# HGRN2 heads of a one-core decoder step: the norm's sum over squares in two rounded parts, and the sample keys spread on the diagonal by ScalarE in place of GpSimd

## The chip, the cores and the metric

The kernel runs on one core of one Trainium2 chip. The metric is the device time of one execution in microseconds (us). The engines are TensorE (PE in the profile, with PEld for its weight loads), VectorE (DVE), ScalarE (ACT), GpSimd (POOL) and SyncE (SP), which issues most of the transfers.

## What is computed

One decoder layer runs for a prompt of 256 tokens and 8 sample tokens together, 264 columns in all. The part that matters here is the recurrence of the eight HGRN2 heads and the norm over each head's output, cut from the reference:

```python
def _rmsnorm(x, g):
    xf = x.astype(jnp.float32)
    y = xf * lax.rsqrt(jnp.mean(xf * xf, axis=-1, keepdims=True) + EPS)
    return (y * g.astype(jnp.float32)).astype(x.dtype)
...
    # S_t = diag(a_t) S_{t-1} + k_t^T v_t, o_t = q_t S_t
    s_new = (jnp.exp(b_last[..., 0, :])[..., None] * s
             + jnp.einsum('bhsk,bhsv->bhkv', ki * jnp.exp(b_last - b), vi))
...
    o_h, s_h = _gated_recurrence(q_h, k_h, i_h, log_f, s_h0)
    o_h = _rmsnorm(o_h, hgrn_norm).astype(h.dtype) * jax.nn.silu(zg).reshape(B, L, HGRN_HEADS, HGRN_DV)
```

Four GLA heads of the same form (128 keys, 256 values) follow the eight HGRN2 heads (128 keys, 128 values). The projections around them multiply 2048 features by some 39,000 columns of weights.

## The kernel before

All activations lie feature-major: 128 features on the partitions, 264 tokens in the free dimension. A weight tile is 2048 x 128 and is cut into two slabs of 128 x 1024. Each slab passes through a ring of four places: SyncE loads it into `raw`, ScalarE rounds it to float32r in `whi` (`round_slab`, L293), VectorE makes the rest `wlo = raw - whi` (`rest_slab`, L298), and TensorE multiplies it (`multiply`, L310 to L312) with three float32r matmuls per 128 x 128 block: high by high, high by low, low by high. ScalarE's rounding waits until the slab four places earlier has been multiplied (semaphore `slabs_multiplied`), so it stands in a fixed distance ahead of TensorE.

In the heads (`head(H, D)` on every engine, D = 1 for an HGRN2 head and D = 2 for a GLA head) the recurrence of one head is laid between the eight slabs of four weight tiles. The order is written out by hand on each engine, and semaphores tie them. TensorE's order in a head is: slabs 0 to 3 with two transposes between 0 and 1, `outer` (L589, eight matmuls, weights `k_diag`, for the sample tokens' state update), slabs 4 and 5, the scores, slab 6, `prob_v`, and slab 7 with `head_norm` and `state` in its middle. ScalarE's `slab(k)` rounds TensorE's slab k + 2, so its `slab(4)` is TensorE's slab 6 and waits for the end of TensorE's slab 2.

Two places are touched. The first is `k_diag`, a 72 x 8 x 128 float32r tile, in which each of the 8 sample tokens' keys stands on its own row and zeros elsewhere. It is `ks_tok` times the column mask `own_row`:

```python
            pool.tensor_tensor(k_diag[:], keys, on_row, ALU.mult).then_inc(h_sem["k_diag_ready"], 1)
```

The second is `head_norm`: ScalarE squares the head's output from PSUM into `sq` (float32), and TensorE sums over the partitions by a matmul with a tile of ones (L645, float32).

Of the kernel before, what the change touches and what calls it, by code (L numbers as in the profile page):

```python
# [28 lines left out]
P = 128  # L29
# [3 lines left out]
NS_TOK = 8  # L33
TOK = NP_TOK + NS_TOK
# [45 lines left out]
F32 = mybir.dt.float32  # L80
F32R = mybir.dt.float32r
ALU = mybir.AluOpType
ACT = mybir.ActivationFunctionType
# [6 lines left out]
def build(nc, t):  # L90
    ctx = ExitStack()

    def sb(name, shape, dt=F32):
        return ctx.enter_context(nc.sbuf_tensor(name, shape, dt))

    def sem(name):
        return ctx.enter_context(nc.semaphore(name))
# [28 lines left out]
    ones = sb("ones", [P, P])  # L126
# [3 lines left out]
    own_row = sb("own_row", [S_ROWS, NS_TOK])  # L130
# [15 lines left out]
    ks_tok = sb("ks_tok", [S_ROWS, P], F32R)  # L146
    vs_tok = sb("vs_tok", [S_ROWS, GDV], F32R)
    k_diag = sb("k_diag", [S_ROWS, NS_TOK, P], F32R)
# [9 lines left out]
    with nc.sbuf_tensor("gate_w", [RANK, GH * P], F32) as gate_w, nc.sbuf_tensor("rank_z", [RANK, TOK], F32) as rank_z:  # L158
        pass
    S = sb("S", [P, 2, 4, GDV])  # L160
    s_out = sb("s_out", [P, GDV])
    sq = sb("sq", [P, 2, TOK])
    rs = sb("rs", [P, TOK])
    o_f = sb("o_f", [P, 2, TOK])
    squares = o_f
# [5 lines left out]
    DG, TP = bank[4], bank[5]  # L171
    O = bank[6:8]
# [34 lines left out]
    by_engine = {  # L207
        "act": ["v_tok_ready", "s_tok_ready", "lev_exp", "kd_exp", "kd_tok_ready", "sq_ready",
                "ln_rs", "rs_ready", "o_hi_done", "s_out_ready", "sg_abs", "sg_exp", "sg_ln", "sg_sigma"],
        "dve": ["s_parts_ready", "lev_sub", "lev_ready", "kd_ready", "s_new0", "s_new1", "masked", "probs_ready", "sg_ls",  # L210
                "sg_ready", "o_scaled", "o_gated", "o_done"],
        "pe": ["v_turned", "s_turned", "outer0", "outer1", "so_done", "scores_done", "kd_turned",
               "pv_done", "state_done", "ss_done"],
# [2 lines left out]
    h_sem = {n: sem(n) for names in by_engine.values() for n in names}  # L216
# [22 lines left out]
    def now(H):  # L239

        return H + 2

    def before(H):

        return H + 1
# [284 lines left out]
    def _(pe):  # L530
# [26 lines left out]
        for h in range(GH):  # L557
            mm = pe.matmul(GATE_BANKS[h][:, 0:TOK], gate_w[:, h * P:(h + 1) * P], rank_z[:], start=True, stop=True)
# [82 lines left out]

        def head_norm(H, D):
            pe.wait_ge(h_sem["sq_ready"], now(H))
            for d in range(D):
                mm = pe.matmul(DG[:, 0:TOK], ones[:], sq[:, d, :], start=d == 0, stop=d == D - 1)  # L645
            mm.then_inc(h_sem["ss_done"], 1)

        def head(H, D):
# [122 lines left out]
    def _(act):  # L771
# [25 lines left out]
        for k in range(KT):  # L797
            if k in X_PARTS:
                act.wait_ge(x_landed[list(X_PARTS).index(k)], 16)
            for to, of in MIRROR:  # L800
                last = act.activation(a_hi[:, k, to], x_in[:, k, of], ACT.Identity, scale=gains[:, 0, k:k + 1])
# [90 lines left out]
        def head(H, D, next_D):  # L892

            T = 4 * H + T_HEADS
            more = next_D is not None

            def slab(k):
                round_slab(act, T + (1 + k // 2), (T_HEADS + 1 + k // 2) % 2, k % 2)

            def exp_gate():  # L900

                act.wait_ge(tiles_drained, T + D)
                act.wait_ge(h_sem["sg_ready"], before(H))
                e = sgl[:, 0:D, :]
                act.activation(e, sgz[:, 0:D, :], ACT.Abs).then_inc(h_sem["sg_abs"], 1)
                act.wait_ge(h_sem["sg_abs"], now(H))
                act.activation(e, e, ACT.Exp, scale=-1.0).then_inc(h_sem["sg_exp"], 1)

            slab(2)
            slab(3)  # L910
            slab(4)
            if D == 1:
                exp_gate()
            slab(5)
            slab(6)
            if D == 2:
                exp_gate()
            slab(7)
            act.wait_ge(h_sem["kd_turned"], now(H))
            act.copy(kd_tok[:], TP[:, 0:2 * P].rearrange("s (b k) -> s b k", b=2)).then_inc(h_sem["kd_tok_ready"], 1)  # L920
            act.wait_ge(h_sem["pv_done"], now(H))
            act.wait_ge(h_sem["ss_done"], before(H))
            for d in range(D):
                sqd = act.activation(sq[:, d, :], O[d][:, 0:TOK], ACT.Square)
            sqd.then_inc(h_sem["sq_ready"], 1)
            slab(8)

            act.wait_ge(h_sem["sg_exp"], now(H))
            act.activation(sgl[:, 0:D, :], sgl[:, 0:D, :], ACT.Ln, bias=ones[:, 0:1]).then_inc(h_sem["sg_ln"], 1)
            act.wait_ge(h_sem["ss_done"], now(H))  # L930
            act.wait_ge(h_sem["probs_ready"], now(H))
            act.wait_ge(h_sem["o_scaled"], before(H))
            act.activation(rs[:], DG[:, 0:TOK], ACT.Ln, scale=1.0 / (D * P), bias=eps_col[:])\
               .then_inc(h_sem["ln_rs"], 1)
            act.wait_ge(h_sem["state_done"], now(H))
            act.wait_ge(state_stored, 16 * H + 16)
            act.copy(s_out[:, 0:D * P], TP[:, 0:D * P]).then_inc(h_sem["s_out_ready"], 1)
            act.wait_ge(h_sem["ln_rs"], now(H))
            act.activation(rs[:], rs[:], ACT.Exp, scale=-0.5).then_inc(h_sem["rs_ready"], 1)
            act.wait_ge(h_sem["sg_ls"], now(H))  # L940
            act.activation(sgl[:, 0:D, :], sgl[:, 0:D, :], ACT.Exp).then_inc(h_sem["sg_sigma"], 1)
            if more:
                slab(9)
                decays(H + 1)
                turned(H + 1, next_D)
            act.wait_ge(h_sem["o_gated"], now(H))
            k = H if D == 1 else 2 * H - HH
            act.copy(b_hi[:, bass.ds(k, D), :], o_f[:, 0:D, :]).then_inc(h_sem["o_hi_done"], 1)
            if not more:
                slab(9)  # L950
# [140 lines left out]
    def _(dve):  # L1091
# [14 lines left out]
        for k in range(KT):  # L1106
            dve.wait_ge(a_hi_ready, k + 1)
            for to, of in MIRROR:
                last = dve.scalar_tensor_tensor(out=a_lo[:, k, to], in0=x_in[:, k, of], scalar=gains[:, 0, k:k + 1],
                                                in1=a_hi[:, k, to].bitcast(F32), op0=ALU.mult, op1=ALU.subtract)  # L1110
# [118 lines left out]
        def head(H, D, more=True):  # L1229
# [3 lines left out]
            def slab(k):  # L1233
                rest_slab(dve, T + (1 + k // 2), (T_HEADS + 1 + k // 2) % 2, k % 2)

            def m_tile(j):

                par = (T_HEADS + j) % 2
                if D == 1:
                    uses = H + HH if par else 2 * H + (HH + (j == 3))  # L1240
                else:
                    uses = H + HH if par else H + 2 * HH
                to_stage(T + j, par, uses)
# [40 lines left out]
            for l in range(LEVELS // 2, LEVELS):  # L1284
                last = level_operands(l)
# [20 lines left out]
            for l in range(1, LEVELS):  # L1306
# [5 lines left out]
                last = dve.tensor_tensor(to, to, of, ALU.add)  # L1312
                last.then_inc(h_sem["probs_ready" if l == LEVELS - 1 else "masked"], 1)
            slab(7)
            m_tile(2)
            if more:
                dve.wait_ge(h_sem["cum_ready"], now(H + 1))
# [16 lines left out]
            for d in range(D):  # L1334
                gain = head_gain[:, (0 if D == 1 else 1 + d):(1 if D == 1 else 2 + d)]
                last = dve.scalar_tensor_tensor(out=o_f[:, d, :], in0=O[d][:, 0:TOK], scalar=gain, in1=rs[:],
                                                op0=ALU.mult, op1=ALU.mult)
# [102 lines left out]
        for j in range(2):  # L1440
            at = part_of(j)
            last = dve.scalar_tensor_tensor(out=ms[:, at], in0=spare(j), scalar=1.0 / D_MODEL, in1=eps_s2[:, at], op0=ALU.mult,
                                            op1=ALU.add)
# [98 lines left out]
    def _(pool):  # L1542
# [41 lines left out]
        for l in range(1, LEVELS):  # L1584
            for side in range(2):
                last = side_masks(l, side)
# [11 lines left out]
        def head(H, D):  # L1598

            pool.wait_ge(h_sem["kd_ready"], before(H))  # L1600
            pool.wait_ge(h_sem["s_new1"], before(H))
            pool.tensor_copy(cum[:, TOK:TOK + 2], totals[:, :, H])
            pool.tensor_copy(cum[:, 0:TOK], gates[:, H, :]).then_inc(h_sem["cum_ready"], 1)
            pool.wait_ge(h_sem["scores_done"], before(H))
            pool.wait_ge(h_sem["so_done"], before(H))
            pool.tensor_copy(q_b[:], zq[:, H, :])
            k = hk[:, H, :] if D == 1 else zk[:, H - HH, :]
            pool.tensor_copy(k_b[:], k)

            pool.wait_ge(v_landed, 16 * H + 16)  # L1610
            pool.wait_ge(h_sem["s_turned"], before(H))
            for i, src in enumerate([k] + [v_st[:, d, :] for d in range(D)]):
                to = s_feat[:, i, :].rearrange("c (g s) -> c g s", g=3)[:, :, 0:NS_TOK]
                column = src[:, NP_TOK:TOK].rearrange("c (o b) -> c o b", o=1).to_broadcast([P, 3, NS_TOK])
                last = pool.tensor_copy(to, column)
            last.then_inc(h_sem["kq_ready"], 1)

            pool.wait_ge(h_sem["s_parts_ready"], now(H))
            pool.wait_ge(h_sem["outer1"], before(H))
            keys = ks_tok[:].bitcast(F32).rearrange("b (o k) -> b o k", o=1).to_broadcast([S_ROWS, NS_TOK, P])  # L1620
            on_row = own_row[:].rearrange("b (c o) -> b c o", o=1).to_broadcast([S_ROWS, NS_TOK, P])
            pool.tensor_tensor(k_diag[:], keys, on_row, ALU.mult).then_inc(h_sem["k_diag_ready"], 1)
# [103 lines left out]
```

## Time and profile before

| | us |
|---|---|
| median of 3 runs | 1679.5 (1678.96 to 1679.57) |
| the profiled execution, its own time | 1679.92 |
| its span | 1678.1 |
| PE busy | 1661.4 (99%) |
| DVE busy | 1095.9 (65%) |
| ACT busy | 808.1 (48%) |
| POOL busy | 202.9 (12%) |

The span is what the profiler saw from the first to the last instruction. About 1.8 us of the execution's own time lie around it. The busy shares are averages over the whole program; the eight HGRN2 heads take 262 to 505 us of it, some 30.4 us each.

### The profile page before, as it was taken

The numbers are of one execution on the slowest core, as the hardware profiler recorded it, in microseconds if no ns is written. First come the engines' busy times: TensorE is split into PE (matmuls) and PEld (weight loads), VectorE is DVE, ScalarE is ACT, GpSimd is POOL, SyncE is SP. The second block draws the span as 40 slices with busy tenths as digits, with TensorE's granted clock in tenths as the row PEclk, the third lists the DMA queues.
The fourth block names the chain that finished last, engine by engine and source line by source line (L and its number), as shares of the span: only waits on it lengthen the run. The fifth ranks groups of instructions, "written<-read, shape, count | busy, mean of one in ns | idle before, by whom it ended". The sixth has DMA issues, their size and how long they took to land.

```text
span 1678.1 us, 36804 instructions
## 1 busy us (share of the span) xinstructions
PE 1661.4 (99%) x13668; PEld 1656.5 (99%) x13668; DVE 1095.9 (65%) x1824; ACT 808.1 (48%) x1102; POOL 202.9 (12%) x196
## 2 busy tenths in 40 slices
PE   7999999999999999999999999999999999999999
PEld 7999999999999999999999999999999999999999
DVE  7558547998988986665697445554455445555775
ACT  7565435556465455543565334443344334443452
POOL 4100001211212110015330000000000000025200
PEclk9999999999999999999999999999999999999999
DMA  9455766575575565775555555555555555565564
GB/s 264 151 188 168 229 203 195 165 218 187 182 226 193 178 216 201 234 262 175 175 177 175 196 179 174 177 192 181 173 179 177 196 177 175 175 197 178 167 191 146
DMA packets 162547, 318.69 MB, mean 190 GB/s; under 512 B 11700, under 2 KB 96436, under 8 KB 162500
## 3 DMA queue, kind: packets, MB, share of 16 engines
q1 hardware_dynamic: 160196, 315.91, 58.6%
q10 hardware_dynamic: 2304, 2.16, 0.4%
q8 instruction: 28, 0.46, 0.1%
q14 instruction: 19, 0.16, 0.0%
HBM read 299.94 MB, written 18.09 MB: 190 GB/s over the span
## 4 chain that ended last, share of the span: by engine, by line
PE 93%; DMA 3%; DVE 2%; issue 1%; ACT 0%; SPq 0%; ACTq 0%; DVEq 0%
PE bank L310 26%; PE bank L311 26%; PE bank L312 26%; PE bank L328 3%; PE bank L330 3%; PE bank L329 3%; DMA lev<-m_spill 3%; PE bank L600 2%; PE bank L613 1%; DVE wlo L298 1%; PE bank L589 1%; PE bank L631 0%; PE bank L645 0%; PE bank L639 0%; DMA raw<-in_stream 0%
## 5 line engine op out<-in xcount | busy, mean ns | idle before, releaser
L293 ACT CAST whi<-raw 128x1024 fp32r<-128x1024 f32 x534 | 548.0, 1048 | 460.1 <-PE bank L312 358.3
L310 PE MATMUL bank<-a_hi,whi 128*128 128x264 f32 x2576 | 737.7, 286 | 0.7 <-DVE wlo L298 0.7
L298 DVE TENSOR_TENSOR wlo<-raw,whi 128x1024 fp32r<-128x1024 f32 x534 | 647.6, 1243 | 137.8 <-ACT whi L293 136.6
L312 PE MATMUL bank<-a_hi,wlo 128*128 128x264 f32 x2576 | 730.3, 284 | 0.0
L311 PE MATMUL bank<-a_lo,whi 128*128 128x264 f32 x2576 | 730.3, 283 | 0.0
L310 PEld LDWEIGHTS bank<-a_hi,whi 128*128 128x128 f32 x2576 | 485.6, 189 | 1.3 <-issue 1.2
L311 PEld LDWEIGHTS bank<-a_lo,whi 128*128 128x128 f32 x2576 | 485.8, 189 | 0.1
L312 PEld LDWEIGHTS bank<-a_hi,wlo 128*128 128x128 f32 x2576 | 483.3, 188 | 0.0
L310 PE MATMUL bank<-b_hi,whi 128*128 128x264 f32 x1280 | 363.5, 284 | 2.0 <-DVE wlo L298 2.0
L311 PE MATMUL bank<-b_lo,whi 128*128 128x264 f32 x1280 | 362.7, 283 | 0.0
L312 PE MATMUL bank<-b_hi,wlo 128*128 128x264 f32 x1280 | 362.7, 283 | 0.0
L310 PEld LDWEIGHTS bank<-b_hi,whi 128*128 128x128 f32 x1280 | 241.2, 188 | 2.2 <-DVE wlo L298 2.2
L311 PEld LDWEIGHTS bank<-b_lo,whi 128*128 128x128 f32 x1280 | 241.3, 188 | 0.0
L312 PEld LDWEIGHTS bank<-b_hi,wlo 128*128 128x128 f32 x1280 | 240.0, 188 | 0.0
L1391 DVE TENSOR_TENSOR room<-room,bank 128x264 f32 x48 | 20.6, 428 | 134.7 <-PE bank L312 134.7
L1047 ACT ACTIVATE lev<-lev 128x264 f32<-128x264 f32 x64 | 27.2, 425 | 167.1 <-DVE lev L1454 167.1
L1555 POOL TENSOR_TENSOR sq<-room 128x264 f32<-128x264 f32 x2 | 2.2, 1084 | 745.0 <-DVE room L1391 620.0
L328 PE MATMUL bank<-b_hi,whi 128*128 128x264 f32 x256 | 73.1, 285 | 0.8 <-DVE b_lo L1103 0.8
L330 PE MATMUL bank<-b_hi,wlo 128*128 128x264 f32 x256 | 72.9, 285 | 0.0
L329 PE MATMUL bank<-b_lo,whi 128*128 128x264 f32 x256 | 72.8, 284 | 0.0
L1460 DVE TENSOR_TENSOR a_lo<-lev,a_hi 128x264 f32 (+1 forms) x64 | 27.3, 432 | 63.0 <-ACT a_hi L1049 63.0
L1393 DVE COPY room<-bank 128x264 f32 (+1 forms) x31 | 13.4, 432 | 80.4 <-PE bank L312 80.4
(178 smaller groups left out, 1542.8 us busy)
## 6 DMA issues: line engine op xcount, KB each, us to landing
raw<-in_stream SPq DMA_DIRECT2D x534, 512.0 KB, 4.3
m_spill<-stage SPq DMA_DIRECT2D x32, 132.0 KB, 5.4
lev<-m_spill SPq DMA_DIRECT2D x16, 264.0 KB, 5.7
S<-in_state_hgrn SPq DMA_DIRECT2D x16, 256.0 KB, 5.4
out_new_hgrn_sample<-S SPq DMA_DIRECT2D x16, 256.0 KB, 4.6
S<-in_state_gla SPq DMA_DIRECT2D x8, 512.0 KB, 7.3
out_new_gla_sample<-S SPq DMA_DIRECT2D x8, 512.0 KB, 5.4
room<-in_x SPq DMA_DIRECT2D x7, 528.0 KB, 7.8
```

The costliest lines, as they stand in the source:

```text
L293: act.copy(whi[:, s, :], raw[:, s, :]).then_inc(hi_ready, 1)
L298: dve.tensor_tensor(wlo[:, s, :], raw[:, s, :], whi[:, s, :].bitcast(F32), ALU.subtract).then_inc(lo_ready, 1)
L310: pe.matmul(out, whi[:, s, w], hi[:, k0 + k, :], start=start and k == 0, stop=False)
L311: pe.matmul(out, whi[:, s, w], lo[:, k0 + k, :], start=False, stop=False)
L312: mm = pe.matmul(out, wlo[:, s, w], hi[:, k0 + k, :], start=False, stop=stop and k == HT - 1)
L328: pe.matmul(out, whi[:, s, w], hi[:, k, :], start=k == 0, stop=False, skip_group_check=True)
L329: pe.matmul(out, whi[:, s, w], lo[:, k, :], start=False, stop=False, skip_group_check=True)
L330: return pe.matmul(out, wlo[:, s, w], hi[:, k, :], start=False, stop=k == KT - 1, skip_group_check=True)
L600: mm = pe.matmul(O[d][:, b:b + 1], S[:, r, i, d * P:(d + 1) * P], q_b[:, b:b + 1], start=(r == 0 and i == 0), stop=True, skip_group_check= ...
L1047: act.activation(u, u, ACT.Square).then_inc(u_ready, 1)
L1391: ins = dve.tensor_tensor(out, out, MM[par][:, 0:TOK], ALU.add)
L1460: dve.tensor_tensor(a_lo[:, T - T0, :], u, a_hi[:, T - T0, :].bitcast(F32), ALU.subtract).then_inc(a_lo_ready, 1)
```

## The change

In HGRN2 heads (D = 1) only: GpSimd no longer makes `k_diag`; ScalarE makes it with eight activations (Identity, each with one column of `own_row` as its scale), put between its `slab(4)` and `exp_gate`. ScalarE squares the head's output twice, into `sq` and, rounded to float32r, into `sq_hi`. VectorE makes `sq_lo = sq - sq_hi` after its `slab(7)` (`sq_lo` lies at the address of `sq`), and TensorE sums both with two float32r matmuls in place of one float32 matmul; the second waits for a new semaphore `sq_parts`.

```diff
@@ TensorE, head_norm
             pe.wait_ge(h_sem["sq_ready"], now(H))
-            for d in range(D):
-                mm = pe.matmul(DG[:, 0:TOK], ones[:], sq[:, d, :], start=d == 0, stop=d == D - 1)
+            if D == 1:
+                pe.matmul(DG[:, 0:TOK], ones[:].bitcast(F32R), sq_hi[:], start=True, stop=False)
+                pe.wait_ge(h_sem["sq_parts"], now(H))
+                mm = pe.matmul(DG[:, 0:TOK], ones[:].bitcast(F32R), sq_lo[:, 0, :], start=False, stop=True)
+            else:
+                for d in range(D):
+                    mm = pe.matmul(DG[:, 0:TOK], ones[:], sq[:, d, :], start=d == 0, stop=d == D - 1)
@@ ScalarE, head
             slab(4)
             if D == 1:
+                act.wait_ge(h_sem["s_parts_ready"], now(H))
+                act.wait_ge(h_sem["outer1"], before(H))
+                for c in range(NS_TOK):
+                    last = act.activation(k_diag[:, c, :], ks_tok[:].bitcast(F32), ACT.Identity, scale=own_row[:, c:c + 1])
+                last.then_inc(h_sem["k_diag_ready"], 1)
                 exp_gate()
...
                 sqd = act.activation(sq[:, d, :], O[d][:, 0:TOK], ACT.Square)
+            if D == 1:
+                sqd = act.activation(sq_hi[:], O[0][:, 0:TOK], ACT.Square)
             sqd.then_inc(h_sem["sq_ready"], 1)
@@ VectorE, head
             slab(7)
+            if D == 1:
+                dve.wait_ge(h_sem["sq_ready"], now(H))
+                dve.wait_ge(h_sem["ss_done"], before(H))
+                dve.tensor_tensor(sq_lo[:, 0, :], sq[:, 0, :], sq_hi[:].bitcast(F32), ALU.subtract)\
+                   .then_inc(h_sem["sq_parts"], 1)
             m_tile(2)
@@ GpSimd, head
             last.then_inc(h_sem["kq_ready"], 1)
 
+            if D == 1:
+                return
             pool.wait_ge(h_sem["s_parts_ready"], now(H))
```

The next two listings are ScalarE's rows around its `slab(4)` in the loop over the HGRN2 heads, first of before. Rows of register instructions stand there too; a name in brackets is a semaphore that the row waits for.

```order
L290 ISA
L292 ISA [waits slab_landed0]
L293 CAST whi<-raw 128x1024 [waits slabs_multiplied]
L902 REGISTER_ALU
L903 REGISTER_ALU [waits tiles_drained]
L905 ACTIVATE room<-room 128x264 [waits sg_ready]
L906 REGISTER_ALU
L907 ACTIVATE room<-room 128x264 [waits sg_abs]
L292 REGISTER_ALU [waits slab_landed1]
L293 CAST whi<-raw 128x1024 [waits slabs_multiplied]
```

And of the changed kernel, whose line numbers are higher:

```order
L293 ISA
L295 ISA [waits slab_landed0]
L296 CAST whi<-raw 128x1024 [waits slabs_multiplied]
L921 REGISTER_ALU
L922 REGISTER_ALU [waits s_parts_ready]
L924 ACTIVATE k_diag<-ks_tok,own_row 72x128 [waits outer1]
L924 ACTIVATE k_diag<-ks_tok,own_row 72x128 x7
L910 REGISTER_ALU
L913 ACTIVATE room<-room 128x264 [waits sg_ready,tiles_drained]
L915 ACTIVATE room<-room 128x264 [waits sg_abs]
```

The eight activations stand directly behind the cast that waits for TensorE's slab 2, and no table load is added. The next two listings are TensorE's rows in the middle of slab 7 of an HGRN2 head, before:

```order
L312 MATMUL bank<-a_hi,wlo 128x264
L645 MATMUL bank<-sq,ones 128x264 [waits sq_ready]
L639 MATMUL bank<-v_tok,kd_tok 128x128 [waits kd_tok_ready]
L639 MATMUL bank<-v_tok,kd_tok 128x128
L310 MATMUL bank<-a_hi,whi 128x264
```

and in the changed kernel:

```order
L315 MATMUL bank<-a_hi,wlo 128x264
L648 MATMUL bank<-sq_hi,ones 128x264 [waits sq_ready]
L650 MATMUL bank<-sq_lo,ones 128x264 [waits sq_parts]
L642 MATMUL bank<-v_tok,kd_tok 128x128 [waits kd_tok_ready]
L642 MATMUL bank<-v_tok,kd_tok 128x128
```

One float32 instruction, which the trace shows as two matmuls, becomes two float32r instructions, of which the second has a wait of its own.

## Rows read from the trace of the kernel before

**Rows 1.** The page's first part: busy time, share of the span, instructions.

```profile
PE 1661.4 (99%) x13668; PEld 1656.5 (99%) x13668; DVE 1095.9 (65%) x1824; ACT 808.1 (48%) x1102; POOL 202.9 (12%) x196
```

**Rows 2.** Waits of PE in the whole span: total us, times, longest.

```profile
PE bank L328 <- DVE wlo L298: 9.7, 1, 9.7
PE bank L310 <- DVE wlo L298: 2.7, 2, 2.0
```

**Rows 3.** Busy time by engine from 262 to 505 us, the HGRN2 heads.

```profile
262.00:505.00 243.00, 243.00 (x2016) 241.84 (x2015) 218.94 (x561) 137.90 (x209) 49.38 (x57) 1.00 0.64 198
```

**Rows 4.** Timeline of ACT in head 3: start, us, instruction, [idle before, releaser].

```profile
354.60 1.05 ACT L293 CAST whi<-raw 128x1024 fp32r<-128x1024 f32 x1 [0.92 <-PE bank L312]
355.56 0.41 ACT L905 ACTIVATE room<-room 128x264 f32<-128x264 f32 x1
...
357.50 1.05 ACT L293 CAST whi<-raw 128x1024 fp32r<-128x1024 f32 x1 [1.07 <-PE bank L312]
361.30 1.05 ACT L293 CAST whi<-raw 128x1024 fp32r<-128x1024 f32 x1 [2.75 <-PE bank L312]
```

**Rows 5.** Timeline of PEld in head 3, the weight loads of outer.

```profile
357.18 0.98 PEld L589 LDWEIGHTS bank<-vs_tok,k_diag 72*128 72x128 f32 x8
```

**Rows 6.** Timeline of POOL in head 3, the product that makes k_diag.

```profile
354.68 1.89 POOL L1622 TENSOR_TENSOR k_diag<-ks_tok,own_row 72x1024 fp32r<-72x1024 f32 x1 [9.36 <-DVE vs_tok L1276]
```

**Rows 7.** ACT groups by shape: busy us, mean ns of one.

```profile
L801 ACT ACTIVATE a_hi<-room,gains 128x128 fp32r<-128x128 f32 x32 | 10.9, 387 | 0.0
L801 ACT ACTIVATE a_hi<-room,gains 128x8 fp32r<-128x8 f32 x16 | 4.6, 286 | 0.0
```

**Rows 8.** Timeline at the start: ACT's triple of L801; DVE's first wlo; PE's first load.

```profile
8.29 1.23 DVE L298 TENSOR_TENSOR wlo<-raw,whi 128x1024 fp32r<-128x1024 f32 x1 [1.72 <-ACT whi L293]
8.49 0.87 ACT L801 ACTIVATE a_hi<-room,gains 128x128 fp32r<-128x128 f32 x3
...
9.63 0.29 PEld L328 LDWEIGHTS bank<-a_hi,whi 128*128 128x128 f32 x1 [9.63 <-issue]
```

**Rows 9.** Timelines of ACT and PEld in the first head.

```profile
263.85 1.05 ACT L293 CAST whi<-raw 128x1024 fp32r<-128x1024 f32 x1 [1.10 <-DMA raw<-in_stream]
265.73 0.98 PEld L589 LDWEIGHTS bank<-vs_tok,k_diag 72*128 72x128 f32 x8
```

**Rows 10.** The same in the last HGRN2 head.

```profile
476.23 1.05 ACT L293 CAST whi<-raw 128x1024 fp32r<-128x1024 f32 x1 [1.09 <-PE bank L312]
478.76 0.98 PEld L589 LDWEIGHTS bank<-vs_tok,k_diag 72*128 72x128 f32 x8
```

**Rows 11.** Timeline of ACT in head 3, behind decays.

```profile
350.32 0.30 ACT L870 ACTIVATE kd<-cum 128x128 f32<-128x128 f32 x1
350.52 0.25 ACT L885 CAST ks_tok<-bank 72x128 fp32r<-72x128 f32 x1
```

**Rows 12.** Timeline of DVE in head 3, while POOL makes k_diag.

```profile
354.98 1.74 DVE L1264 TENSOR_TENSOR lev<-lev,q_b 128x128 f32<-128x128 f32 x1
356.65 0.28 DVE L1265 TENSOR_TENSOR lev<-lev,k_b 128x128 f32<-128x128 f32 x1
```

**Rows 13.** Timeline of PE in head 3, around head_norm.

```profile
373.17 0.29 PE L312 MATMUL bank<-a_hi,wlo 128*128 128x264 f32 x1
373.29 0.61 PE L645 MATMUL bank<-sq,ones 128*128 128x264 f32 x2
373.74 0.61 PE L639 MATMUL bank<-v_tok,kd_tok 128*128 128x128 f32 x4
```

**Rows 14.** Timelines of ACT, DVE and PEld in head 3, around the squares.

```profile
372.03 0.39 ACT L924 ACTIVATE sq<-bank 128x264 f32<-128x264 f32 x1 [5.01 <-PE bank L632]
372.32 1.04 ACT L293 CAST whi<-raw 128x1024 fp32r<-128x1024 f32 x1
372.08 0.42 DVE L1128 TENSOR_TENSOR stage<-bank,r_bc 128x264 f32<-128x264 f32 x1
373.18 0.31 PEld L645 LDWEIGHTS bank<-sq,ones 128*128 128x128 f32 x2
```

More of the change, by code:

```diff
@@ L161, in build @@
     s_out = sb("s_out", [P, GDV])
+    with nc.sbuf_tensor("sq_lo", [P, 2, TOK], F32R) as sq_lo:
+        pass
     sq = sb("sq", [P, 2, TOK])
+    sq_hi = sb("sq_hi", [P, TOK], F32R)
     rs = sb("rs", [P, TOK])
@@ L209, in build @@
                 "ln_rs", "rs_ready", "o_hi_done", "s_out_ready", "sg_abs", "sg_exp", "sg_ln", "sg_sigma"],
-        "dve": ["s_parts_ready", "lev_sub", "lev_ready", "kd_ready", "s_new0", "s_new1", "masked", "probs_ready", "sg_ls",
+        "dve": ["s_parts_ready", "lev_sub", "lev_ready", "kd_ready", "s_new0", "s_new1", "sq_parts", "masked", "probs_ready", "sg_ls",
                 "sg_ready", "o_scaled", "o_gated", "o_done"],
```

## The prediction
> **What bounds the kernel now.** I read the page first: TensorE is busy 99% of the span, VectorE 65%, ScalarE 48%, GpSimd 12% [rows 1]. A share of 99% says that little but TensorE's own work can shorten the program, and that any wait put into TensorE's queue is paid in full. The waits of PE say the same: the two largest are 9.7 and 2.7 us, together 12.4 us in 1678 [rows 2]. Then I cut out the eight HGRN2 heads, since the change touches only them. From 262 to 505 us TensorE is busy for 243.00 of 243.00 us, VectorE for 218.94 (90%), ScalarE for 137.90 (57%) and GpSimd for 49.38, and the clock is granted in full [rows 3]. So in this stage TensorE is the bound, VectorE is nearly as full but is not waited for, and ScalarE has room on average. The reader should not stop at the average. ScalarE rounds slabs in a ring of four, so its cast in the middle of a head starts when TensorE ends slab 2, and whatever is queued behind this cast stands at a fixed distance ahead of TensorE. The timeline of one head shows that distance, and it decides this case.
>
> **The change, part by part.** The first part is `k_diag`. TensorE wants it at the weight loads of `outer`, which in head 3 start at 357.18 [rows 5]. Before, GpSimd starts the product at 354.68, directly after VectorE has written the keys' rests, takes 1.89 us and ends at 356.57, 0.6 us early [rows 6]. After, ScalarE makes it, and the eight activations stand behind the cast of its `slab(4)`. This cast starts at 354.60, after 0.92 us in which ScalarE waited for TensorE, and the instruction behind it starts at 355.56, 0.96 later [rows 4]. The other waits of the first activation are over by then: the keys' rests are there before 354.68, where GpSimd started on them [rows 6].
>
> What do eight activations take? The trace has the same form in another place: Identity with a column as scale, 128 elements to a partition, float32 in and float32r out. One takes 387 ns, and one with 8 elements 286 ns [rows 7]. Three in a row (128, 128 and 8 elements) take 0.87 us [rows 8], so two starts follow each other by (0.87 - 0.286)/2 = 0.29 us. That these run over 128 partitions and the new ones over 72 I take as no difference. Eight take 7 x 0.29 + 0.387 = 2.42 us. The last one ends 0.96 + 2.42 = 3.38 us after the start of the cast. From the end of a producer to TensorE's weight load that waited for it the trace shows 9.63 - (8.29 + 1.23) = 0.11 us [rows 8]. So the weight load of `outer` can start 3.49 us after the cast's start. Before, it starts 357.18 - 354.60 = 2.58 us after it [rows 4, 5]. TensorE waits 0.91 us in this head.
>
> It is not recovered. The cast of the next head again starts when TensorE has ended its slab 2, so the distance is the same in each head. Heads 1 to 6 have this distance within 0.02 us, all six. The last head has 478.76 - 476.23 = 2.53 us, hence a wait of 0.96 [rows 10]. In the first head the cast came later, since it waited for its slab's transfer: 265.73 - 263.85 = 1.88 us, hence a wait of 1.61 [rows 9]. The sum is 6 x 0.91 + 0.96 + 1.61 = 8.0 us.
>
> From below, the cost is bounded by an activation without a column operand: the next instruction starts 350.52 - 350.32 = 0.20 us after it, and it takes 0.30 [rows 11]. Eight take 7 x 0.20 + 0.30 = 1.70, the waits are 0.19 in six heads, 0.24 and 0.89, in sum 2.3 us. From above I add 0.1 us per head, about one matmul's start distance, for TensorE's restart after an idle time: 8.8 us. I take 8.0, because its row has the same function, operand and element types.
>
> The second part is the norm's sum. Before, one float32 matmul shows as two of 128 x 264, and from the first one's start to the next instruction's start are 373.74 - 373.29 = 0.45 us [rows 13]. A float32r matmul of the same width starts 0.12 us before the next one (373.17 to 373.29) [rows 13], so two take 0.24. The saving is 0.21 us per head, 1.7 us in eight.
>
> The second of these matmuls now waits for VectorE. ScalarE's first square starts at 372.03 and the next instruction 0.29 later; a second square from the same bank ends at 372.32 + 0.39 = 372.71. VectorE's subtraction then needs about 0.42, the price of its 264-column operation at 372.08, and ends near 373.15 (with a start some 0.02 after ScalarE's end) [rows 14]. With 0.11 to TensorE the load could go at 373.26. The first of the two loads stands at 373.18 and the second would follow 0.12 later, at 373.30 [rows 13, 14]. That is a margin of 0.04 us, so I cost the wait at nothing, and at up to 0.15 us per head, 1.2 us in all, if it is gone. The distances are counted from TensorE's own `prob_v`, which releases the squares, so they hold whatever the wait at `outer` has done before.
>
> The rest is covered. ScalarE gets 0.29 us more for the second square, taken from the 0.92 us that it waits before the cast [rows 4]. Its next cast, at 357.50, moves to 355.56 + 8 x 0.29 = 357.88 for the activations, plus 0.86 for `exp_gate` (two operations of some 0.43), near 358.7. The cast behind it at 361.30 had 2.75 us of idle time ahead of it [rows 4], and TensorE multiplies the late slab as its slab 7, more than 10 us on. VectorE stands in its queue for the squares (it was free at 372.08, and would go on after 373.15, about 1.1 us later [rows 14]). Behind it are `m_tile(2)`, the level differences and the slabs of the next head.
>
> VectorE gets time back as well. Its operation at L1264 takes 1.74 us where L1265, of the same size, takes 0.28, and it ends at 356.72, 0.15 after GpSimd's product [rows 6, 12]. Both read two operands from SBUF. Without GpSimd's product this operation should cost some 0.3, and VectorE gains 1.4 us in each head, which pays for the wait at the squares. For the time it gives nothing, since TensorE did not wait for VectorE here [rows 3].
>
> The Trainium skill, page "SBUF — State Buffer", section "SBUF: two separate sides", has the rule: VectorE operations with two SBUF inputs and GpSimd operations that read SBUF take one shared pair of ports as an exclusive lock, and the loser blocks for the whole instruction. The trace agrees (1.74 us against 0.28). By that rule alone, this change ought to make the kernel faster; it is a rival below.
>
> **The sum.** 8.0 - 1.7 = +6.3 us. The profiled execution took 1679.92 us, so it would take 1686.2. It lies 0.4 above the median of the runs, so I predict 1685.8 us, 0.38% slower. What a measurement of this kernel can tell from no change is about 0.2%, or 3.4 us.
>
> **Rivals.**
> - The activations are cheap. If the column operand costs nothing, the waits come to 2.3 us, and with the saving the time is 1680.1, no change. For it: an average ScalarE load of 57%. Against it: 387 against 300 ns in the two rows of 128 elements. It decides at a start distance p where 6w + (w + 0.05) + (w + 0.7) = 5.1, hence w = 0.54 us. With w = 0.96 + 7p + (p + 0.1) + 0.11 - 2.58, p = 0.24 us. Above that the kernel is slower by more than 0.2%.
> - VectorE's relief shows. If TensorE were held by VectorE in these heads, 1.46 us in each would come back, 11.7 us in eight, and with the saving and no late `k_diag` the time would be 1666.1. Against it stand 243.00 busy of 243.00 us [rows 3]; and even then `k_diag` must be in time. The rule of the Trainium skill's page "SBUF — State Buffer" stands behind this rival.
> - No wait at all: `k_diag` is in time and only the saving is left, 1677.8, a gain of 0.1% that is no change by the bound. The same rows as above speak against it, since it needs 2.58 us for 3.49.
> - Late second norm matmul: the wait for `sq_parts` comes to 0.15 us per head on top of the forecast, 1687.0. Only 0.04 us of margin speak against it.
>
> **How the numbers follow.** The forecast has 0.75, the forecast with the late norm matmul 0.10. The cheap activations have 0.10 and no wait at all 0.03, both no change. VectorE's relief has 0.02. So slower 0.85, same 0.13, faster 0.02. The range reaches from 1683.0 (a start distance of about 0.25 us) to 1688.0 (the restart cost of 0.8 and the norm's wait of 1.2 both added to 1685.8, rounded up). It leaves out the cases of no change and of a gain.
>
> **What would show it.** In the profile of the changed kernel, the waits of PE should have a row of the weight load or matmul of `outer` waiting for ScalarE's `k_diag`, eight times, 7 to 9 us in all, 1.6 the longest. ScalarE's timeline should show eight activations in about 2.4 us directly behind the cast. The two norm matmuls should start 0.12 us apart, with no or a tiny wait for `sq_lo`. L1264's operation should fall to some 0.3 us in the HGRN2 heads and stay at 1.74 in the GLA heads. I am wrong if the activations follow each other by 0.2 us or less, or if TensorE had reserve that I don't see between slab 2 and `outer`.

## The result and the profile after

| | before | changed |
|---|---|---|
| median, us | 1679.22 (1675.83 to 1680.24, 7 runs) | 1684.1 (1682.18 to 1686.04, 7 runs) |
| ratio | | 1.0033 (95% interval 1.0024 to 1.0043) |
| profiled execution, own time | 1679.92 | 1684.1 |
| its span | 1678.1 | 1682.3 |

The change makes the kernel slower by 4.9 us. The forecast was 1685.8, with a range from 1683.0 to 1688.0. The ratios here and below are estimated from the fast runs alone and differ by up to 0.05% from the quotients of the medians shown.

The first part of the changed kernel's page answers to [rows 1]. TensorE is as busy as before; ScalarE has 20 us more and GpSimd 20 us less.

```profile
PE 1662.9 (99%) x13668; PEld 1657.1 (98%) x13668; DVE 1089.8 (65%) x1832; ACT 828.1 (49%) x1174; POOL 183.1 (11%) x188
```

The waits of PEld, TensorE's weight loads, in the changed kernel (in all us, times, longest). The second row is new: eight waits of the loads of `outer` for ScalarE's keys.

```profile
PEld bank L331 <- issue: 9.0, 1, 9.0
PEld bank L592 <- ACT k_diag L924: 7.2, 8, 1.5
PEld bank L331 <- DVE b_lo L1118: 1.0, 1, 1.0
PEld bank L592 <- POOL k_diag L1644: 0.7, 3, 0.2
PEld bank L313 <- issue: 0.7, 2, 0.3
PEld bank L313 <- DVE wlo L301: 0.4, 1, 0.4
```

Head 3 in the timelines of ACT and PEld answers to [rows 4, 5]. The cast starts at 357.84, the eight activations 0.95 later, and they take 2.45 us. The first load of `outer` starts at 361.29. That is 3.45 us after the cast, where it was 2.58.

```profile
357.84 1.05 ACT L296 CAST whi<-raw 128x1024 fp32r<-128x1024 f32 x1 [0.45 <-PE bank L315]
358.79 2.45 ACT L924 ACTIVATE k_diag<-ks_tok,own_row 72x128 fp32r<-72x128 f32 x8
361.29 0.97 PEld L592 LDWEIGHTS bank<-vs_tok,k_diag 72*128 72x128 f32 x8 [0.80 <-ACT k_diag L924]
392.31 0.97 PEld L592 LDWEIGHTS bank<-vs_tok,k_diag 72*128 72x128 f32 x8 [0.80 <-ACT k_diag L924]
```

I call the time from one first load of `outer` to the next head's the head period. It is 392.31 - 361.29 = 31.02 us here, and was 387.60 - 357.18 = 30.42 before (30.37 to 30.44 in heads 1 to 6, all told about 30.40). The next head's load before is this row of PEld:

```profile
387.60 0.98 PEld L589 LDWEIGHTS bank<-vs_tok,k_diag 72*128 72x128 f32 x8
```

A head costs 0.6 us more. Its wait is 0.80 and its distance grows by 0.87, so about 0.2 us comes back from the norm. In the same head the norm's two matmuls lie 0.12 us apart, with no wait ahead of either (timeline of PE, against [rows 13]). VectorE's operation that stood beside GpSimd's product (L1264 before, L1279 now) has a mean of 769 ns over the twelve heads, where it had 1744: it is short in the eight HGRN2 heads and as long as before in the four GLA heads.

```profile
377.34 0.28 PE L648 MATMUL bank<-sq_hi,ones 128*128 128x264 f32 x1
377.47 0.28 PE L650 MATMUL bank<-sq_lo,ones 128*128 128x264 f32 x1
377.59 0.61 PE L642 MATMUL bank<-v_tok,kd_tok 128*128 128x128 f32 x4
```

### The profile page after: what moved, and what is told of

It is laid out like the page before. It is cut to its first block, busy times and chain, and to the rows that moved or that the text cites. A ratio compares the mean times of both kernels' runs of the same rounds, so it can differ in the third digit from the quotient of the medians.

```text
span 1682.3 us, 36877 instructions
## 1 busy us (share of the span) xinstructions
PE 1662.9 (99%) x13668; PEld 1657.1 (98%) x13668; DVE 1089.8 (65%) x1832; ACT 828.1 (49%) x1174; POOL 183.1 (11%) x188
## 4 chain that ended last, share of the span: by engine, by line
PE 86%; ACT 5%; DMA 3%; issue 3%; DVE 2%; ACTq 0%; SPq 0%; DVEq 0%
PE bank L313 24%; PE bank L314 24%; PE bank L315 24%; PE bank L331 3%; PE bank L333 3%; PE bank L332 3%; DMA lev<-m_spill 3%; PE bank L603 2%; ACT k_diag L924 1%; PE bank L616 1%; ACT whi L296 1%; DVE wlo L301 1%; PE bank L592 1%; ACT lev L874 1%; DMA raw<-in_stream 1%
```

## The experiments

Medians stand against the kernel before, which ran beside each run on the same chip. The head period is read from one profile of each run, between the first loads of `outer` in two neighbouring heads, so nothing that happens outside the heads is in it.

| run | median, us | before, us | ratio (95% interval) | head period, us |
|---|---|---|---|---|
| changed, first time | 1684.1 | 1679.22 | 1.0033 (1.0024 to 1.0043) | 31.02 |
| e1, keys on ScalarE only | 1686.8 | 1678.74 | 1.0053 (1.0039 to 1.0067) | 31.22 |
| e2, norm in two parts only | 1681.19 | 1678.74 | 1.0013 (1.0004 to 1.0022) | 30.69 |
| e3, no column operand | 1678.75 | 1678.74 | 1.0004 (0.9995 to 1.0013) | 30.28 |
| e4, keys ahead of the cast | 1681.11 | 1678.74 | 1.0011 (1.0002 to 1.002) | 30.67 |
| e5, keys on VectorE, short norm | 1679.64 | 1678.49 | 1.0005 (0.9996 to 1.0014) | 30.70 |
| e6, keys behind the gate | 1698.5 | 1678.49 | 1.0116 (1.0101 to 1.0132) | 31.9 or 33.44 |
| e7, keys on VectorE, old norm | 1678.37 | 1678.49 | 0.9999 (0.999 to 1.0009) | 30.37 |
| e8, keys in two halves | 1676.14 | 1678.49 | 0.9991 (0.9982 to 1.0) | 30.23 |
| e9, changed again | 1685.56 | 1678.86 | 1.0038 (1.0024 to 1.0052) | 31.02 |
| e10, e6 again (one execution) | 1700.31 | 1678.86 | none | 31.9 or 33.45 |
| e11, e8 and a product on VectorE | 1678.92 | 1678.74 | 1.0 (0.9991 to 1.001) | 30.42 |
| e8 again | 1675.81 | 1678.74 | 0.9986 (0.9977 to 0.9995) | 30.23 |

The theory was that the loss sits in ScalarE's queue: whatever stands between the cast that TensorE releases and the last key is paid by TensorE at `outer`. The rivals were that VectorE's or the norm's new wait, or the clock, makes the loss.

**e1: one part alone.** The norm is as before.

```diff
@@ the changed kernel, ScalarE, VectorE and TensorE
-                sqd = act.activation(sq_hi[:], O[0][:, 0:TOK], ACT.Square)
...
-                dve.tensor_tensor(sq_lo[:, 0, :], sq[:, 0, :], sq_hi[:].bitcast(F32), ALU.subtract)
...
-                pe.matmul(DG[:, 0:TOK], ones[:].bitcast(F32R), sq_hi[:], start=True, stop=False)
-                mm = pe.matmul(DG[:, 0:TOK], ones[:].bitcast(F32R), sq_lo[:, 0, :], start=False, stop=True)
+                mm = pe.matmul(DG[:, 0:TOK], ones[:], sq[:, d, :], start=d == 0, stop=d == D - 1)
```

> Only the keys move to ScalarE; the norm keeps its one float32 matmul. Theory (the keys stand behind a cast whose start TensorE sets, so the weight loads of outer come 3.45 us after that cast and not 2.58): the same wait of TensorE for ScalarE's k_diag as in the changed kernel, 7 to 7.5 us in eight heads, a head period of 31.27 us (30.40 + 0.87), and a time some 2 us above the changed kernel's, since the norm's saving of 0.25 us a head is gone: 8 to 9 us over the kernel before, ratio about 1.005. Rival (part of the loss comes from the norm's new wait or from VectorE standing for the squares): less than the changed kernel's loss of 4.9 us.

The loss is 8.1 us by the medians and 8.9 by the ratio, about as expected, and larger than that of the whole change. Two loads of `outer` from e1's timeline of PEld, one period of 31.22 us apart, show the same 0.80 us of waiting:

```profile
359.92 0.97 PEld L592 LDWEIGHTS bank<-vs_tok,k_diag 72*128 72x128 f32 x8 [0.80 <-ACT k_diag L919]
391.14 0.97 PEld L592 LDWEIGHTS bank<-vs_tok,k_diag 72*128 72x128 f32 x8 [0.80 <-ACT k_diag L919]
```

The loss is the keys', and the short norm takes 31.22 - 31.02 = 0.20 us a head off it. So in the changed kernel the norm doesn't lose.

**e2: the other part alone.** GpSimd makes the keys.

```diff
@@ the changed kernel, ScalarE and GpSimd
-                    last = act.activation(k_diag[:, c, :], ks_tok[:].bitcast(F32), ACT.Identity, scale=own_row[:, c:c + 1])
...
-            if D == 1:
-                return
```

> Only the norm is summed in two parts; GpSimd makes the keys. Theory: no wait of TensorE in the heads, a head period of 30.15 us (30.40 less 0.25), 2 us below the kernel before, ratio about 0.9988. VectorE's operation at the side of GpSimd's product stays at 1.74 us, and VectorE loses about 1.3 us a head to the wait for the squares and the subtraction. Rival (VectorE has no room for that, since it frees prob_v only 0.14 us ahead of TensorE in the kernel before): TensorE waits for VectorE's pairs or wlo, up to 1 us a head, and the time is 4 to 8 us above the kernel before.

My expectation failed. I looked for 2 us of gain, and the run is slower by 0.13%; the rival was right in kind, but it said 4 to 8 us and the run is some 2 us slower. The waits of PEld in e2:

```profile
PEld bank L582 <- issue: 1.9, 7, 0.3
PEld bank L634 <- DVE pairs L1322: 1.7, 8, 0.2
```

The second row is VectorE. In the kernel before the pairs for `prob_v` were late in the first head alone (0.20 us), and now they are 0.21 us late in each head. The first row is the transpose of the samples, which waits for GpSimd's `kq_ready` (the waits of PE in e5 name GpSimd's `s_feat` there). In e2's timeline of POOL, the copy ahead of that signal takes 3.30 us; in the kernel before it took 0.26 to 0.76 in the same seven heads. The first row is of the kernel before, the others are of e2.

```profile
374.81 0.50 POOL L1615 COPY s_feat<-before_b 128x24 f32 x1 [3.93 <-DMA v_st<-v_spill]
375.82 3.30 POOL L1630 COPY s_feat<-before_b 128x24 f32 x1 [4.44 <-DMA v_st<-v_spill]
379.06 0.20 POOL L1630 COPY s_feat<-v_st 128x24 f32<-128x24 f32 x1
```

It ends where VectorE ends a row of operations on two SBUF operands (timeline of DVE in e2: the last of them is at 378.76, and a gap of 0.79 us follows).

```profile
378.76 0.29 DVE L1212 TENSOR_TENSOR lev<-cum 128x128 f32<-128x128 f32 x1
379.84 1.23 DVE L301 TENSOR_TENSOR wlo<-raw,whi 128x1024 fp32r<-128x1024 f32 x1 [0.79 <-ACT whi L296]
```

**e3: the price of the column.** The sample tokens' state update gets other numbers here, since each activation writes all the keys.

```diff
-                    last = act.activation(k_diag[:, c, :], ks_tok[:].bitcast(F32), ACT.Identity, scale=own_row[:, c:c + 1])
+                    last = act.activation(k_diag[:, c, :], ks_tok[:].bitcast(F32), ACT.Identity)
```

> As the changed kernel, but the eight activations have no column as scale: each writes all the keys, so the sample tokens' state update gets other numbers, with the same instructions otherwise. Theory (the price is eight starts behind the cast, 0.29 us each with a column, 0.20 without): the eight take 1.7 us, the weight loads of outer come 2.75 us after the cast, TensorE waits about 0.15 us a head, head period 30.3 us, time within 1 us of the kernel before. Rival (the column costs nothing, the time is in the tile's form): 2.44 us for the eight as in the changed kernel and its time, 1684.

The timeline of ACT in e3: eight activations in 1.71 us in place of 2.45.

```profile
354.53 1.05 ACT L296 CAST whi<-raw 128x1024 fp32r<-128x1024 f32 x1 [0.44 <-PE bank L315]
355.49 1.71 ACT L924 ACTIVATE k_diag<-ks_tok 72x128 fp32r<-72x128 f32 x8
```

The time is that of the kernel before, as expected. The trace names no wait at `outer` but in the first head; the load there starts 357.25 - 354.53 = 2.72 us after the cast, and I had expected 2.75. So 0.74 us a head, nearly the whole wait, is the price of eight column operands.

**e4: ahead of the cast.**

```diff
+            if D == 1:
+                (the two waits and the eight activations)
             slab(4)
             if D == 1:
-                (the two waits and the eight activations)
                 exp_gate()
```

> As the changed kernel, but the eight activations stand ahead of ScalarE's slab(4), behind slab(3), so they wait for VectorE's rests of the keys and no longer for TensorE's slab 2. Theory: they start near the time at which the cast starts now and end 2.42 us later, so outer's weight loads come with a wait of 0 to 0.3 us a head instead of 0.80, head period 30.2 to 30.4 us, the cast comes 2.4 us later with no wait of TensorE for it, time 0 to 2 us below the kernel before. Rival (ScalarE is full here, and the later cast or gate delays wlo or the next head's decays): TensorE waits for wlo or lev instead, and the time stays near 1684.

The wait falls from 0.80 to 0.45 us, not to 0 to 0.3, and the time ends 0.11% above the kernel before. The activations no longer wait for TensorE but for VectorE's rests of the keys. Those come later against TensorE than before, since ScalarE has a second square ahead of them (0.29 us) and TensorE is 0.2 us faster. In head 3 ScalarE's cast of `ks_tok` starts 2.98 us after the load of the samples' transpose (351.27 - 348.29), where in the kernel before it was 2.49 (350.52 - 348.03). I had left both out of this expectation. The period is 388.63 - 357.96 = 30.67 us.

```profile
357.96 0.97 PEld L592 LDWEIGHTS bank<-vs_tok,k_diag 72*128 72x128 f32 x8 [0.45 <-ACT k_diag L923]
388.63 0.97 PEld L592 LDWEIGHTS bank<-vs_tok,k_diag 72*128 72x128 f32 x8 [0.45 <-ACT k_diag L923]
```

**e8: two halves.** To e4 I added a signal after the first four activations, since the first four matmuls of `outer` need no more.

```diff
+                    if c == 3:
+                        last.then_inc(h_sem["k_half_ready"], 1)
@@ TensorE, outer
-                pe.wait_ge(h_sem["k_diag_ready"], now(H))
+                pe.wait_ge(h_sem["k_half_ready" if D == 1 else "k_diag_ready"], now(H))
+            elif D == 1:
+                pe.wait_ge(h_sem["k_diag_ready"], now(H))
```

> As the run with the activations ahead of the cast, and the first four of them release the first four matmuls of outer, the last four the others. Theory: there the eight came 0.45 us late; the first four are now in time, and the last four are wanted 0.44 us later than before, so the wait falls to 0 to 0.1 us a head, period 30.2 to 30.3, time 1 to 2 us below the kernel before. Rival (the loop over the squares and pairs is the bound at 30.4 or more whatever the keys do): a wait at the pairs or at the transpose of the samples appears in place of that at outer, period 30.4 to 30.7.

> The run with the keys in two halves once more beside it: period 30.22 us without a long copy on GpSimd, 1 to 3 us below the kernel before.

This is the fastest version. No wait at `outer` is left in the HGRN2 heads, the period is 416.50 - 386.27 = 30.23 us (timeline of PEld in the second run), and the ratios are 0.9991 and 0.9986.

```profile
386.27 1.04 PEld L594 LDWEIGHTS bank<-vs_tok,k_diag 72*128 72x128 f32 x8
416.50 1.04 PEld L594 LDWEIGHTS bank<-vs_tok,k_diag 72*128 72x128 f32 x8
```

TensorE gets in full what the short norm saves, some 0.2 us a head. The first interval ends at 1.0 and the second at 0.9995, so the gain of some 2 to 3 us is seen, but only just. In the two profiles the way from the first to the eighth `outer` is 1.3 us shorter than before (211.72 and 211.69 us against 213.03); where the rest of the gain lies was not looked for.

**e5 and e7: the keys on VectorE,** with the short and with the old norm.

```diff
+            if D == 1:
+                dve.wait_ge(h_sem["s_parts_ready"], now(H))
+                dve.wait_ge(h_sem["outer1"], before(H))
...
+                dve.tensor_tensor(k_diag[:], keys, on_row, ALU.mult).then_inc(h_sem["k_diag_ready"], 1)
```

> The norm in two parts as in the changed kernel, but VectorE makes the keys of the HGRN2 heads with one product of 72 x 1024, directly behind its rests of the keys. Theory (two things bound a head: TensorE's own work, 30.15 us with the short norm, and a loop ScalarE squares, ScalarE up to its cast, VectorE's rests, its operands and pairs, TensorE's prob_v, squares again, whose length in the kernel before is just under 30.40; VectorE's product of some 1.2 us takes the place of 1.46 us that it stood beside GpSimd's): no wait at outer, L1264's operation at 0.28 us, head period 30.15 to 30.35 us, time 0 to 2 us below the kernel before. Rival (VectorE has no room for another product): TensorE waits for the pairs by 0.3 us a head or more, period above 30.6, time 2 us or more above the kernel before.

> The kernel before with one edit: VectorE makes the keys, GpSimd does not; the norm is the float32 matmul. Theory: the port is free, L1264's operation falls from 1.74 to 0.28 us, and still the time doesn't move, since TensorE's own work of 30.4 us a head is the bound: ratio 0.999 to 1.001, period 30.38 to 30.42. Rival (VectorE's standing beside GpSimd costs time): 5 to 10 us below the kernel before.

The groups of DVE by shape in e5: the product costs 1221 ns. The operation that stood beside GpSimd's product has a mean of 770 ns over twelve heads, because it is 1745 in the four GLA heads and 282 in the eight others.

```profile
L1293 DVE TENSOR_TENSOR k_diag<-ks_tok,own_row 72x1024 fp32r<-72x1024 f32 x8 | 9.8, 1221 | 1.0
L1274 DVE TENSOR_TENSOR lev<-lev,q_b 128x128 f32<-128x128 f32 x12 | 9.2, 770 | 0.0
```

VectorE gains 1.46 us in a head, and spends 1.22 and a wait of 0.13 again. With the old norm nothing moves (0.9999, period 30.37): TensorE's own work bounds the head. With the short norm, e5 has e2's waits again, 0.21 us at the pairs and 0.27 at the transpose, in seven of eight heads, and e2's period. My expectation of 30.15 to 30.35 failed. The rival's period came (above 30.6), though its time didn't: it said 2 us or more above the kernel before, and the run is 0.8 to 1.2 us above. VectorE has no room for this product when the norm is short.

**e11: VectorE loaded again.** To e8 I added a product that nobody needs.

```diff
+                dve.wait_ge(h_sem["s_parts_ready"], now(H))
...
+                dve.tensor_tensor(probs[0:S_ROWS], keys, on_row, ALU.mult)
```

> As the run with the keys in two halves (head period 30.22 us, no wait), with one product more on VectorE behind its rests of the keys, 72 x 896 into a tile that is overwritten later in the head; nobody needs its result. It takes some 1.1 us with a wait of 0.1 to 0.15 ahead of it, nearly what VectorE got back when GpSimd's product went (1.46 us). Theory (the short norm can be had only while VectorE has that time back): TensorE waits for the pairs again in each head, 0.05 to 0.25 us, and the head period is 30.45 to 30.7. Rival (the wait at the pairs in the norm-only run came from something else, as GpSimd's late copy of the samples): no wait at the pairs and a period of 30.22.

The period rises from 30.23 to 30.42 and the gain is gone (1.0), but not by the wait that I named. There is none at the pairs; the transpose of the samples waits some 0.28 us, eight times (timelines of PEld and POOL in e11).

```profile
376.67 0.15 PEld L582 LDWEIGHTS bank<-ident,s_feat 128*72 128x72 f32 x2 [0.28 <-issue]
373.11 3.29 POOL L1645 COPY s_feat<-before_b 128x24 f32 x1 [4.19 <-DMA v_st<-v_spill]
```

All eight copies from the first head to the eighth are long (3.16 to 3.88 us). In each of the two runs of e8 one copy of seven is long (3.8 and 3.88 us), and that head's period is 30.49 and 30.47 in place of 30.2. In e5 the one head without it has 30.44 and the others 30.7 to 30.8. So a long copy costs TensorE about 0.25 us. VectorE's relief is needed for the gain, and it works in part through GpSimd's copy.

**e6 and e10: more ahead of the keys.**

```diff
+                exp_gate()
                 (the two waits and the eight activations)
-                exp_gate()
```

> As the changed kernel, but the eight activations stand behind exp_gate, two operations of 0.41 and 0.43 us, and not ahead of it. Theory (what is queued ahead of the keys is paid in full by TensorE at outer): outer's weight loads come about 4.3 us after the cast and not 3.45, the wait is 1.65 us a head and not 0.80, period 31.85 to 31.9, time some 7 us above the changed kernel's, ratio to the kernel before about 1.0075. Rival (there is reserve in the ring behind the keys, or the clock and not the wait makes the loss): less than 3 us above the changed kernel.

> The run with the keys behind the gate once more: the wait at outer is 1.68 us in each head again; if the clock's fall behind it is chance, the heads in which it falls are not the same ones, and each such head is 1.5 us longer than the others (33.4 against 31.9).

The wait is what was expected: 1.68 us a head, and 2.47 in the first. Two operations of 0.4 us ahead of the keys are paid in full, so the ring holds no reserve. The timeline of PEld in e6:

```profile
332.60 0.97 PEld L592 LDWEIGHTS bank<-vs_tok,k_diag 72*128 72x128 f32 x8 [1.68 <-ACT k_diag L925]
364.50 0.97 PEld L592 LDWEIGHTS bank<-vs_tok,k_diag 72*128 72x128 f32 x8 [1.68 <-ACT k_diag L925]
```

These two are 31.90 us apart, as expected. But the time is 14 us above the changed kernel's and not 7. Four of the seven periods are 33.44, 1.54 us longer, and in each of them TensorE's clock fell (below); it fell a fifth time behind the wait of the last head. Waits of 14.3 us in place of 7.2, and five falls in place of one, are some 13 us. In e10 the period behind the first head is 35.03 us, and of the other six, three are 33.44 to 33.46 and not all in e6's places. So the heads in which it falls are chance. That it falls is not: the mean granted clock was 0.995 or 0.996 in all four executions of e6 and 0.994 in that of e10.

**e9: the changed kernel again.**

> The changed kernel once more, for two things that its first profile leaves open. Its first head ran 15 matmuls at a start distance of 0.22 us and not 0.12 behind a wait of 1.54 us (the granted clock fell to half, some 1.5 us lost), and TensorE waited only 0.4 us for VectorE's wlo in the phase behind the heads, where all other profiles have 1.6 to 3.4. If both are chance, the same waits at outer come back (1.5 to 1.6 once, 0.80 seven times, head period 31.02), the wait behind the heads is near 2, and the clock may or may not fall. If they belong to the change, both come back. Time: 4.5 to 7 us above the kernel before.

The waits came back exactly (1.60 once, 0.80 to 0.86 seven times, period 31.02), and so did the fall of the clock in the first head. The small waits behind the heads (0.4 us in the first profile) were 1.0 here, with 0.6 to 3.4 in the others. They vary by themselves and don't belong to the change.

## Why the prediction was right

**The wait at outer** was right in mechanism and nearly in size. I forecast 3.49 us from the cast's start to the load, and it is 3.45; 2.42 us for eight activations, and they take 2.44 to 2.45; waits of 0.91, 0.96 and 1.61, and they are 0.80, 0.86 and 1.54 by the trace. In sum 7.2 us against 8.0. Some 0.06 us a head more are lost between the wait and full speed: the distance grew by 0.87 where the trace names 0.80. e3 shows the column operand's price and e6 that nothing absorbs a delay.

**It isn't recovered** was right: the period is 31.02 us five times and 31.08 once from head 1 on, and in e9 31.02 five times and 31.07.

**The norm's saving** was right: 0.21 forecast, 0.20 from e1 against the changed kernel. No wait appears at `sq_parts` in any profile. But the margin was smaller than my 0.04 us: in the changed kernel the load of the second matmul starts 0.07 to 0.11 us after VectorE's subtraction ends, about the 0.11 us that I took from a producer's end to a load. The term was nothing by a hair.

**VectorE's relief** was right as costed, at nothing by itself: e7 has it, less a new product, and stays at 0.9999 with the old norm. It was incomplete as an argument. I wrote that the relief "pays for the wait at the squares" and gives nothing for the time. e2 shows what it pays: without it the short norm costs time. The two parts of the change don't add. The norm alone makes a head 0.29 us longer, the keys alone 0.82, and both 0.62. The Trainium skill's page "SBUF — State Buffer", section "SBUF: two separate sides", gives an exclusive lock of the shared ports as the reason why VectorE's operation stands beside GpSimd's product; the trace agrees (1745 ns beside it, 282 without).

**The rivals.** Cheap activations would have given 1680.1; e3 made them cheap and got the kernel before's time (1.0004). Late `sq_parts` did not come.

**What was missed.** The clock's fall in the first head, 1.54 us, was in no term. In the profiled executions two things outside my sum offset it: TensorE started 0.7 us earlier (9.0 us of waiting against 9.7) and waited 2.3 us less for `wlo` behind the heads. Both vary as much between the other profiles, so I call them chance. Added up: distance 6 x 0.87 + 0.92 + 1.6 = 7.7, norm -1.6, clock +1.5, chance -3.0 makes 4.6, and the spans differ by 4.2. So part of the agreement is luck in this one profile. The ratio of e9, 1.0038 or 6.4 us, is nearer to the forecast of 6.3; its interval and that of the first measurement overlap. The fall isn't in every execution: a mean granted clock of 0.999 or less, which one such fall gives, stands in 7 of the 12 of the changed kernel (both measurements) and in 20 of the 82 of the kernel before that ran beside the experiments at a full or nearly full clock. An estimate from these is (7/12 - 20/82) x 1.54 = 0.5 us of the loss.

**Still open.** Each long copy on GpSimd ends with a run of VectorE's operations, but why one copy gets in between two of them and another waits for the end of the run isn't shown: no run moved the copy alone.

## What to carry to other kernels

Ask of each new operation what releases the instruction ahead of it in its queue. ScalarE had 43% idle time in this stage, and still every tenth of a microsecond behind one cast was paid, since TensorE sets that cast's start. Where an operation's result is wanted in pieces, signal the pieces: a signal after four of eight activations, ahead of the cast, turned a loss of 0.3% into a gain of 0.1%, little as that is. And a saving on the bounding engine is had only while the next engine has room, so try the parts of a change alone and together.

## What the runs showed of the hardware

**The clock fell after a short wait.** The changed kernel by stretches of the first head: PE, PEld, DVE, ACT and POOL busy, each with its number of instructions in brackets, and behind these the granted clock (1.00, 0.93, 0.50, 0.71, 1.00), DMA share and GB/s.

```profile
262.00:266.00 4.00, 3.36 (x28) 3.15 (x26) 3.92 (x15) 2.82 (x9) 0.00 (x0) 1.00 0.75 275
266.00:268.00 2.00, 1.31 (x10) 1.31 (x11) 2.00 (x11) 1.97 (x6) 0.00 (x0) 0.93 0.41 113
268.00:270.00 2.00, 2.00 (x11) 2.00 (x10) 2.00 (x9) 0.34 (x1) 0.00 (x0) 0.50 0.44 158
270.00:272.00 2.00, 2.00 (x14) 2.00 (x13) 2.00 (x2) 0.00 (x0) 1.87 (x1) 0.71 0.00 0
272.00:274.00 2.00, 2.00 (x19) 2.00 (x18) 1.16 (x3) 1.05 (x1) 0.62 (x2) 1.00 0.69 190
```

TensorE had been busy without a gap, waited 1.54 us up to 266.69, and about 1 us after it went on the granted clock was 0.50, the lower level of 1.2 GHz. It stayed there for some 3.4 us. The timeline of PE there shows matmuls 0.22 us apart and 0.42 long, and from 271.16 on 0.12 and 0.28 again.

```profile
270.72 0.42 PE L315 MATMUL bank<-a_hi,wlo 128*128 128x264 f32 x1
270.94 0.38 PE L313 MATMUL bank<-a_hi,whi 128*128 128x264 f32 x1
271.16 0.29 PE L314 MATMUL bank<-a_lo,whi 128*128 128x264 f32 x1
271.28 0.28 PE L315 MATMUL bank<-a_hi,wlo 128*128 128x264 f32 x1
```

Some 15 matmuls at the lower level cost 15 x 0.10 = 1.5 us, as much as the wait itself. Behind the waits at `outer`, it came after those of 1.54 and 1.60 us (changed kernel, e9) and after ten of the sixteen of 1.65 to 2.47 us (five each in e6 and e10; in the first head of e10 it lasted twice as long and cost 3.1 us). It didn't come after the 1.61 us of e1, the 2.47 us of e6's first head, nor any of the 21 waits of 0.80 to 0.86 us.

It isn't bound to the heads. Behind the heads, near 650 us (later in e6 and e10), TensorE waits once for `wlo` in every profile. In those of e2, e4, e5, e7 and e11 this wait was 1.8 to 2.6 us and the clock fell behind it. In the kernel before, e1, e3, e6 and the first run of e8 it was 1.6 to 2.5 and the clock stayed, as it did in the other four, where the wait was 0.2 to 0.9. So whether a fall follows a wait of 1.5 to 2.6 us is, as far as these runs show, chance, and it adds some 1.5 us to an execution whatever the run was made to test. For differences of 1 to 3 us the head periods are the safer reading. The stretches of e2:

```profile
648.00:650.00 2.00, 0.04 (x1) 0.05 (x1) 1.97 (x6) 1.17 (x2) 0.00 (x0) 1.00 0.41 159
650.00:652.00 2.00, 2.00 (x11) 2.00 (x12) 1.77 (x4) 1.72 (x3) 0.00 (x0) 0.60 0.33 102
652.00:654.00 2.00, 2.00 (x11) 2.00 (x11) 1.97 (x6) 1.13 (x2) 0.00 (x0) 0.55 0.84 266
654.00:656.00 2.00, 2.00 (x19) 2.00 (x18) 1.25 (x2) 0.00 (x0) 0.00 (x0) 1.00 0.83 287
```

**GpSimd can stand for a whole run of VectorE's operations.** A copy of 24 elements to a partition took 0.2 to 0.8 us in most heads and 1.0 to 1.2 in some. In 24 cases of the HGRN2 heads (7 in e2, 7 in e5, 8 in e11, one in each run of e8) it took 2.7 to 3.9 us, and each of these ended 0.05 to 0.07 us after the end of a run in which VectorE had no pause; 9 to 13 of its operations began while the copy stood. It isn't enough that the copy starts inside such a run. The two copies below are of the first run of e8. VectorE ran without a pause to 406.66 and to 437.10 us, the first copy ends with that run and the second doesn't.

```profile
402.92 3.80 POOL L1640 COPY s_feat<-before_b 128x24 f32 x1 [3.68 <-DMA v_st<-v_spill]
432.90 0.35 POOL L1640 COPY s_feat<-before_b 128x24 f32 x1 [3.22 <-DMA v_st<-v_spill]
```
